# A fused two-block transformer kernel on one core: the gate products of the second block's mixers are spread over the attention, on a ring of six slots

## The chip, the cores and the metric

The kernel runs on one core of a Trainium2 chip. Everything is computed in float32. The metric is the time of one execution in microseconds of the device; the kernel before takes 2779.77 us (median of three runs, 2775.85 to 2779.93).

## The reference, cut to what matters

Two blocks follow each other on 256 tokens of 1024 features. The first (two linear recurrences and a mixture of 32 experts) isn't touched by the change. The second has two layers; each is a feed-forward half step, a mixer and another feed-forward half step. The change lies in the mixer:

```python
h = rmsnorm(x, norm_mix[l])
qa, ka, va, qb_, kb, vb, qc, kc, vc, gate_logits = jnp.split(h @ w_in[l], split_points, axis=-1)
y_a = mixer_a(...)   # 8 heads of 64: q and k normed and rotated (rope), plain softmax
y_b = mixer_b(...)   # 8 heads of 64: relative bias, window mask, and a sink logit in the softmax
y_c = mixer_c(...)   # 4 heads of 2 x 64: p = softmax(first) - lam * softmax(second), values of 128, norm
ys = jnp.stack([y_a, y_b, y_c], axis=2)                              # 3 branches of 512
branches = jnp.einsum('bsnw,nwd->bsnd', ys, w_branch[l])             # 3 x (512 -> 1024)
gates = jax.nn.sigmoid(gate_logits.reshape(b, s, N_BRANCH, D_MODEL)) # 3 x (1024 -> 1024)
merged = jnp.sum(gates * branches, axis=2)
x = x + merged @ w_out[l]
```

## The kernel before, in words

All weights stream from memory in 446 blocks of 1 MB, in the order that `stream_order` (L63) writes down. SyncE loads block i into a slot of a ring of 12 (`place`, L108); it waits on the count `w_used` until TensorE has freed the block that was in the slot. `take` (L491) is TensorE's side: the next block, once it has landed. Six slots are buffers of their own, the other six are one buffer, `ring_late`. Each engine's program is written out by hand, in its own order, with semaphores between them. On ScalarE the helper `act` (L2009) waits for its own result after each instruction.

A float32 matmul of the source is two instructions in the trace, so a product of 128 x 128 weights with 256 columns shows as two matmuls and two weight loads.

The mixer on TensorE (`mixer`, L1101) does, one after the other:

1. The projections: 8 blocks of q and k with 256 columns each (`project`, tiles of two matmul groups in the banks `pj`, which ScalarE copies out), then v from two blocks.
2. The rope of branch A: ScalarE squares q and k, TensorE sums them over a head (`rope_sums`), VectorE scales (`rope_gained`), TensorE rotates (`rope_rotated`), VectorE and ScalarE finish with eight passes over five tiles. The scores wait for the last of them (`rope_done`).
3. The attention: 24 maps of 256 x 256 scores in 20 units (16 units of one map in A and B, 4 units of two maps in C). For unit u TensorE does the scores of u, the transposes of unit u-2 (`turn`, four of 128 x 128, L513) and the values of unit u-3. For each map VectorE copies the scores out of PSUM or adds the bias (L1876, L1879), takes the row maximum (L1881), negates it (L1889), and after ScalarE's two exponentials divides by the sum (L1902). Scores use 64 rows of the array, the values of A and B 64 columns.
4. The norm of branch C (`c_squared`, `c_sums`, `c_variance`, `c_inverse`, `y_ready`).
5. `merge` (L872): for each of 3 branches and 4 pairs of feature tiles one branch tile (8 products of 256 columns) and one gate tile (16 products). ScalarE copies the first and puts the second through the sigmoid, VectorE multiplies and adds.
6. The output product, 4 blocks with 512 columns, into four banks.

The bias tiles (3 MB) are read back from memory by two transfers on ScalarE's queue at the start of each mixer, since their place is used by the feed-forward steps between.

The feed-forward steps (`feed_forward`, L1056) use a seven-product scheme: 11 steps "up" of two blocks each, whose weights VectorE combines partly in place in the ring (`weights_up`, L1676), and 11 steps "down" of one block.

## Time and profile before

| what | us |
|---|---|
| median of the runs | 2779.77 |
| runs shown | 2775.85, 2779.77, 2779.93 |
| span of the profiled execution, first to last instruction | 2773.7 |
| TensorE busy in it | 2550.8 |
| VectorE busy | 1103.4 |
| ScalarE busy | 585.4 |

No total time is given for the profiled execution beside its span; its span lies 6.1 us under the median of the runs. The mixer of the first layer begins at 1449 us of the span and its output product ends at 1784.6 us; that of the second lies between 2217 and 2553 us.

### The profile page before, as it was taken

What the parts mean: (1) busy time and instruction counts of PE and PEld (TensorE: products, weight loads), DVE (VectorE), ACT (ScalarE), POOL (GpSimd) and SP (SyncE); (2) the same over time, 40 slices, a digit from 0 to 9 for tenths busy, and PEclk for the clock granted to TensorE, in tenths of its full rate; (3) what the DMA queues carried; (4) which work ended last, traced back from release to release, by engine and by line L of the source; (5) the groups of instructions that cost most, each with busy time, mean ns of one, the idle gap of its engine ahead of it and who ended that gap; (6) DMA issues with size and microseconds to landing.
All of it is one profiled execution on the core that took longest, in us unless ns stands there. A gap on an engine that the chain in (4) does not pass through costs nothing.

```text
span 2773.7 us, 37722 instructions
## 1 busy us (share of the span) xinstructions
PE 2550.8 (92%) x15259; PEld 1933.4 (70%) x15264; DVE 1103.4 (40%) x2325; ACT 585.4 (21%) x1032; POOL 115.3 (4%) x98
## 2 busy tenths in 40 slices
PE   5999889989799999979999779999999997799998
PEld 2686588868456655549948468699499484586993
DVE  1455445501311111136550831366666507312665
ACT  3632422210211111121011521110100105311000
POOL 0000144300000000000000000000000000000000
PEclk8999999999999999989999889999999998799999
DMA  7126100025499999974444004344344350043340
GB/s 280 62 79 278 54 31 1 1 108 211 157 414 422 422 422 422 422 309 173 178 147 173 30 1 182 152 166 184 142 162 176 144 196 31 1 182 152 153 168 15
DMA packets 74309, 485.50 MB, mean 175 GB/s; under 512 B 7872, under 2 KB 14528, under 8 KB 16704
## 3 DMA queue, kind: packets, MB, share of 16 engines
q1 hardware_dynamic: 65808, 472.46, 42.8%
q10 hardware_dynamic: 8368, 11.14, 1.2%
q8 instruction: 98, 1.61, 0.2%
q14 instruction: 35, 0.29, 0.0%
HBM read 479.38 MB, written 4.19 MB: 174 GB/s over the span
## 4 chain that ended last, share of the span: by engine, by line
PE 82%; DVE 7%; DMA 5%; ACT 3%; issue 2%; SPq 0%; ACTq 0%; DVEq 0%; POOL 0%; POOLq 0%
PE bank L501 80%; DMA ring<-in_stream 5%; ACT arena L2010 2%; PE bank L513 2%; DVE arena L1191 1%; DVE softmax_small L1881 1%; DVE arena L1879 1%; DVE arena L1902 0%; ACT hT L2010 0%; DMA bias_scratch<-arena 0%; ACT ring_late L2010 0%; DVE arena L1449 0%; ACT L2010 0%; DVE softmax_small L1889 0%; DVE arena L1485 0%
## 5 line engine op out<-in xcount | busy, mean ns | idle before, releaser
L501 PE MATMUL bank<-arena 128*128 128x128 f32 (+4 forms) x3864 | 619.5, 318 | 67.8 <-ACT arena L2010 43.1
L501 PEld LDWEIGHTS bank<-arena 128*128 128x128 f32 (+2 forms) x3864 | 485.4, 195 | 175.5 <-issue 87.0
L501 PE MATMUL bank<-hT,ring 128*128 128x256 f32 (+2 forms) x2144 | 463.3, 374 | 8.1 <-issue 6.7
L2010 ACT ACTIVATE arena<-bank 128x512 f32<-128x512 f32 (+2 forms) x384 | 218.0, 568 | 1156.7 <-PE bank L501 1131.2
L501 PEld LDWEIGHTS bank<-hT,ring 128*128 128x128 f32 x2144 | 357.5, 193 | 97.1 <-issue 64.7
L501 PE MATMUL bank<-ring,arena 128*64 128x256 f32 (+3 forms) x2184 | 298.6, 406 | 31.3 <-DMA ring<-in_stream 29.0
L501 PE MATMUL bank<-hT,ring_late 128*128 128x256 f32 (+1 forms) x1568 | 279.4, 336 | 6.7 <-issue 6.7
L501 PEld LDWEIGHTS bank<-ring,arena 128*64 128x64 f32 (+2 forms) x2184 | 176.4, 141 | 144.7 <-issue 82.7
L501 PEld LDWEIGHTS bank<-hT,ring_late 128*128 128x128 f32 x1568 | 248.9, 193 | 31.0 <-issue 7.5
L2010 ACT ACTIVATE hT<-bank 128x256 f32<-128x256 f32 (+2 forms) x92 | 38.6, 420 | 642.4 <-PE bank L501 471.3
L501 PE MATMUL bank<-arena,ring_late 128*128 128x128 f32 (+1 forms) x1088 | 157.4, 299 | 5.1 <-DVE arena L1485 2.8
L501 PE MATMUL bank<-ring_late,hT 128*64 128x512 f32 (+2 forms) x632 | 162.0, 584 | 0.0
L1191 DVE TENSOR_TENSOR arena<-arena 128x512 f32<-128x512 f32 (+5 forms) x55 | 33.7, 615 | 321.4 <-ACT arena L2010 320.8
L501 PEld LDWEIGHTS bank<-arena,ring_late 128*128 128x128 f32 x1088 | 144.2, 193 | 12.7 <-DVE arena L1485 3.6
L513 PE MATMUL bank<-constants,arena 128*128 128x128 f32 x492 | 87.1, 325 | 58.3 <-ACT arena L2010 44.5
L501 PE MATMUL bank<-arena,ring 128*128 128x128 f32 (+1 forms) x864 | 125.0, 299 | 11.5 <-issue 8.0
L513 PEld LDWEIGHTS bank<-constants,arena 128*128 128x128 f32 x492 | 68.1, 167 | 93.1 <-issue 58.0
L1191 DVE TENSOR_TENSOR arena<-arena,bank 128x512 f32<-128x512 f32 x16 | 11.0, 688 | 303.7 <-PE bank L501 303.7
L501 PEld LDWEIGHTS bank<-arena,ring 128*128 128x128 f32 x864 | 114.1, 195 | 17.7 <-issue 12.7
L501 PEld LDWEIGHTS bank<-ring_late,hT 128*64 128x64 f32 (+1 forms) x632 | 58.1, 147 | 87.8 <-issue 85.0
L501 PE MATMUL bank<-ring_late,arena 128*64 128x256 f32 (+2 forms) x680 | 115.7, 404 | 3.2 <-DVE arena L1513 2.3
L2001 POOL TENSOR_TENSOR x_tok<-x_tok,arena 128x512 f32<-128x512 f32 x8 | 11.8, 1492 | 2207.2 <-DVE arena L1802 2207.2
(215 smaller groups left out, 2239.1 us busy)
## 6 DMA issues: line engine op xcount, KB each, us to landing
ring<-in_stream SPq DMA_DIRECT2D x248, 1024.0 KB, 8.9
ring_late<-in_stream SPq DMA_DIRECT2D x198, 1024.0 KB, 10.4
arena<-bias_scratch ACTq DMA_DIRECT2D x4, 1536.0 KB, 18.0
bias_scratch<-arena ACTq DMA_DIRECT2D x12, 256.0 KB, 2.0
constants<-in_con SPq DMA_DIRECT2D x1, 1184.0 KB, 9.3
x_tok<-in_x SPq DMA_DIRECT2D x1, 1024.0 KB, 5.3
arena<-in_ctx SPq DMA_DIRECT2D x1, 1024.0 KB, 6.8
out<-x_tok SPq DMA_DIRECT2D x2, 512.0 KB, 2.7
```

The lines of the kernel that those rows point to most:

```text
L501: ins = engine.matmul(out_, lhsT, rhs, start=start, stop=stop, skip_group_check=True)
L513: ins = engine.transpose(out_, in_, ident[0:k, 0:k])
L1191: return tt(o, x, y, ALU.mult)
L1879: tt(e, src, bias2[:, m.bias], ALU.add).then_inc(*v.inc("sm_in"))
L1881: engine.tensor_reduce(stat(m, 0), e, AX.X, ALU.max).then_inc(*v.inc())
L2001: engine.tensor_tensor(x, x, ffU[j], ALU.add).then_inc(*g.inc("ff_joined"))
L2010: engine.activation(o, i, f, **kw).then_inc(*s_.inc(ev))
```

## The change

Parts of the second block alone are changed.

- **Ring.** From the end of the experts on, blocks go through six slots and not twelve. `ring_slots` makes a table of each block's slot, its use count and the block that was there before it. `ring_late` is free from there on: its first half holds the gates of a mixer (`gates2`, 24 tiles of 256 columns), its second half the bias tiles, which are now loaded once, on ScalarE's queue right behind the experts.
- **Stream.** The order is now all 12 gate blocks, then the 6 branch blocks, then the 4 output blocks.
- **Rope.** It is woven into the projections: sums and rotation stand on TensorE behind the fourth of the eight q and k tiles, and v comes last.
- **Attention.** It goes in 12 steps of two maps. In each TensorE does the scores of both maps, alternating between the two row halves; the first half of one gate tile; the transposes of the step before; the second half of the gate tile; and the values of the step before, alternating between the two column halves. ScalarE copies the gate logits into `gates2`.
- **Softmax.** VectorE takes maximum and bias in one instruction per 128 x 256 half for B and C (`tensor_tensor_reduce`, listed as ISA, with a read of the accumulator), and reduces straight from PSUM for A; the copy and the negation are gone. The sink is a 257th column of the exponential.
- **Branches last.** 12 branch tiles in banks 2 and 3 alternately, multiplied by VectorE straight from PSUM with the gates. The last step's transposes stand behind the first branch tile and its values behind the second. ScalarE does the sigmoids as four instructions of 1024 columns before the norm of C and two behind it.

The diff, cut to its core:

```diff
+def ring_slots():
+    slots = [i % (RING if EARLY <= i < MOE_LAST else HALF_RING) for i in range(N_BLOCKS)]
...
-                    back = HALF_RING if i < EARLY + HALF_RING else RING
-                    if i >= back:
-                        sp.wait_ge(sem("w_used"), i - back + 1)
+                    if before(i) >= 0:
+                        sp.wait_ge(sem("w_used"), before(i) + 1)
...
             def mixer(l, turned):
-                project(8, LAT, turned)
-                w = [take(), take()]
-                project_tok([(lambda k, t_=t_: hT[:, k, NC + 128 * t_:NC + 128 * t_ + 128]) for t_ in range(2)], w)
-                engine.wait_ge(*pe.at("pj_free", state["tile"]))
+                steps = project_steps(8, LAT, turned)
+                for _ in range(3):
+                    next(steps)
                 engine.wait_ge(*pe.at("lam_product", l + 1))
                 mm(bank[7][:, 256:258], ..., ev="lam_sums")
+                next(steps)
...
+                for _ in steps:
+                    pass
+                w = [take(), take()]
+                project_tok([(lambda k, t_=t_: hT[:, k, NC + 128 * t_:NC + 128 * t_ + 128]) for t_ in range(2)], w)
...
+                def scores(t):
+                    pair = MAPS[2 * t:2 * t + 2]
+                    for m in pair:
+                        if m.n >= 3:
+                            scores_free(m.n - 3)
+                    for qb in range(2):
+                        for m in pair:
                             a0, a1 = m.lanes
                             mm(bank[2 + m.n % 3][:, 256 * qb:256 * qb + 256], qT[a0:a1, m.q, 128 * qb:128 * qb + 128],
                                (kc if m.kc else kab)[a0:a1, m.k, :], start=True, stop=True, ev="sm_scores" if qb else None)
...
-                for u in range(N_UNITS + 3):
-                    if u < N_UNITS:
-                        scores(u)
-                    if 2 <= u < N_UNITS + 2:
-                        turn(u - 2)
-                    if u >= 3:
-                        values(u - 3)
+                def branch_tile(i, w):
+                    b, m2 = divmod(i, 4)
+                    if i < 2:
+                        for n in (N_MAPS - 3, N_MAPS - 2, N_MAPS - 1):
+                            scores_free(n)
+                    else:
+                        engine.wait_ge(*pe.at("merge_used", 8 + 12 * l + i - 1))
+                    if b == 2 and m2 == 0:
+                        engine.wait_ge(*pe.at("y_ready", 3 + l))
+                    t = bank[2 + i % 2]
...
+                for t in range(N_SLOTS):
+                    scores(t)
+                    gate = gate_tile()
+                    gate_half(gate, 0)
+                    if t:
+                        turn(t - 1)
+                    gate_half(gate, 1)
+                    if t:
+                        values(t - 1)
+                for b in range(3):
+                    w = [take(), take()]
+                    for m2 in range(4):
+                        if b == 0 and m2 == 1:
+                            turn(N_SLOTS - 1)
+                        if b == 0 and m2 == 2:
+                            values(N_SLOTS - 1)
+                        if b == 1 and m2 == 0:
+                            engine.wait_ge(*pe.at("c_squared", l + 1))
...
+                        branch_tile(4 * b + m2, w)
...
-                    if m.bias is None:
-                        engine.tensor_copy(e, src).then_inc(*v.inc("sm_in"))
...
-                    engine.tensor_reduce(stat(m, 0), e, AX.X, ALU.max).then_inc(*v.inc())
...
+                    for qb in range(2):
+                        engine.tensor_tensor_reduce(e[:, qb, 0:256], src[:, qb, :], bias2[:, m.bias, qb, :], -1.0, sink,
+                                                    ALU.add, ALU.min, stat(m, 0)[:, qb:qb + 1]).then_inc(*v.inc("sm_max" if qb else None))
...
+                def branch_tile(i):
+                    b, m2 = divmod(i, 4)
+                    engine.wait_ge(*v.at("br_full", 12 * l + i + 1))
+                    if i in (0, 8):
+                        engine.wait_ge(*v.at("gates_ready", 2 * l + i // 8 + 1))
+                    o, g, src = mrg2[:, 2 * m2:2 * m2 + 2, :], gates2[:, 2 * i:2 * i + 2, :], psum(2 + i % 2, 2)
...
                 act(csq, y4, ACT.Square, "c_squared")
+                for i in range(4):
+                    act(gates2[:, 4 * i:4 * i + 4, :], gates2[:, 4 * i:4 * i + 4, :], ACT.Sigmoid, "gates_ready" if i == 3 else None)
                 engine.wait_ge(*s_.at("c_variance", l + 1))
                 act(csq, csq, ACT.Ln)
                 act(csq, csq, ACT.Exp, "c_inverse", scale=-0.5)
-                merge(3, 8 + 12 * l, eg2, brs2)
+                for i in range(4, 6):
+                    act(gates2[:, 4 * i:4 * i + 4, :], gates2[:, 4 * i:4 * i + 4, :], ACT.Sigmoid, "gates_ready" if i == 5 else None)
```

How the order of the instructions moves, at three places. The names of the waits are those of semaphores that are used a second time: `gla_scores` is `sm_scores`, `gla_arg` `sm_max`, `gla_exp` `sm_exp`, `gla_products` `sm_p`, `dn_p` `sm_turned`, `dn_p_copied` `sm_pt`, `dn_y` `sm_pv`, `dn_d` `sm_o`; `gla_merged` is `sm_in` before and `br_full` now; `dn_u_copied` is `lam_product`, `dn_at_copied` `rope_squared`, `dn_x0` `lam_read`, `dn_a` `rope_gained`.

TensorE, attention of the first layer, before: one unit of branch A in the steady state.

```order
L501 MATMUL bank4<-arena 128x256 [waits gla_merged]
L501 MATMUL bank4<-arena 128x256
L513 MATMUL bank6<-constants,arena 128x128 [waits dn_p_copied,gla_products]
L513 MATMUL bank6<-constants,arena 128x128 x3
L501 MATMUL bank7<-arena 64x256 [waits dn_d,dn_p_copied]
L501 MATMUL bank7<-arena 64x256
```

The same place now: one step of two maps.

```order
L524 MATMUL bank3<-arena 128x256 [waits gla_exp]
L524 MATMUL bank4<-arena 128x256
L524 MATMUL bank3<-arena 128x256
L524 MATMUL bank4<-arena 128x256
L524 MATMUL bank0<-hT,ring1 128x256 [waits landed1,pj_free]
L524 MATMUL bank0<-hT,ring1 128x256 x7
L536 MATMUL bank5<-constants,arena 128x128 [waits gla_products,dn_p_copied]
L536 MATMUL bank5<-constants,arena 128x128 x3
L536 MATMUL bank6<-constants,arena 128x128 [waits gla_products]
L536 MATMUL bank6<-constants,arena 128x128 x3
L524 MATMUL bank0<-hT,ring1 128x256 x8
L524 MATMUL bank7<-arena 64x256 [waits dn_d,dn_p_copied]
```

Sixteen gate products came between the scores, the transposes and the values, eight on each side of the transposes.

TensorE, from the last attention step of the first layer into the branch tiles, now (bank 2 and bank 3 are the branch tiles):

```order
L524 MATMUL bank2<-hT,ring5 128x256 [waits gla_arg,landed0,landed5]
...
L536 MATMUL bank6<-constants,arena 128x128 [waits gla_products,dn_p_copied]
L536 MATMUL bank6<-constants,arena 128x128 x3
L524 MATMUL bank3<-hT,ring5 128x256 [waits gla_arg]
...
L524 MATMUL bank7<-arena 128x256 [waits dn_d,dn_p_copied]
L524 MATMUL bank7<-arena 128x256
L524 MATMUL bank2<-hT,ring5 128x256 [waits merge_used]
```

The third branch tile stands behind the last values, and it needs the bank of the first.

ScalarE at the same place, now: from the copy of the last transposes (into `arena`) and the last values to the last sigmoids.

```order
L2097 ACTIVATE arena<-bank6 128x512 [waits dn_p,dn_y,dn_d]
L2097 ACTIVATE arena<-bank7 128x256 [waits dn_y,dn_p_copied]
L2097 ACTIVATE arena<-arena 128x1024 [waits dn_d]
ACT_TABLE_LOAD
L2097 ACTIVATE ring_late<-ring_late 128x1024 [waits c_squared]
L2097 ACTIVATE ring_late<-ring_late 128x1024 [waits act] x3
ACT_TABLE_LOAD [waits c_variance]
L2097 ACTIVATE arena<-arena 128x1024 [waits gates_ready]
ACT_TABLE_LOAD
L2097 ACTIVATE arena<-arena 128x1024 [waits act]
ACT_TABLE_LOAD
L2097 ACTIVATE ring_late<-ring_late 128x1024 [waits c_inverse]
```

The four sigmoids behind which `gates_ready` is raised come after the square of branch C, and four table loads stand here; before, the merge had one.

## Rows read from the trace of the kernel before

**Rows 1.** The page: the span, and the busy time of each engine.

```profile
span 2773.7 us, 37722 instructions
PE 2550.8 (92%) x15259; PEld 1933.4 (70%) x15264; DVE 1103.4 (40%) x2325; ACT 585.4 (21%) x1032; POOL 115.3 (4%) x98
```

**Rows 2.** Busy time of the engines in stretches: the first layer's mixer, and some of the second's.

```profile
core 0: us, PE busy (x) PEld busy (x) DVE busy (x) ACT busy (x) POOL busy (x), PEclk, DMA share, GB/s
1449.00:1518.40 69.40, 69.30 (x323) 60.69 (x320) 0.94 (x3) 6.14 (x11) 0.00 (x0) 1.00 0.54 197
1518.40:1535.30 16.90, 7.74 (x14) 3.73 (x14) 9.99 (x16) 4.82 (x6) 0.00 (x0) 0.76 0.34 124
1535.30:1617.20 81.90, 64.31 (x256) 37.67 (x256) 64.94 (x172) 50.01 (x144) 0.00 (x0) 0.82 0.00 1
1617.20:1627.00 9.80, 1.98 (x4) 0.68 (x4) 4.02 (x7) 3.17 (x3) 0.00 (x0) 0.79 0.00 0
1627.00:1640.00 13.00, 12.95 (x46) 10.96 (x47) 0.00 (x0) 0.60 (x1) 0.00 (x0) 0.77 0.01 1
1640.00:1756.80 116.80, 114.58 (x531) 100.51 (x529) 13.84 (x20) 16.31 (x25) 0.00 (x0) 1.00 0.33 133
```

**Rows 3.** The chain that ended last: start us, us, what.

```profile
1570.86 0.70 DVE arena L1879
1571.58 0.70 DVE softmax_small L1881
1574.21 0.70 DVE arena L1879
...
1627.05 127.54 PE bank L501 x576
...
1756.85 27.75 PE bank L501 x64
...
2217.22 69.08 PE bank L501 x320
...
2525.06 27.75 PE bank L501 x64
```

**Rows 4.** Groups by form in the attention, 1535.4 to 1617 us.

```profile
L2010 ACT ACTIVATE arena<-arena,softmax_small 128x256 f32<-128x256 f32 x48 | 24.4, 508 | 25.1 <-DVE softmax_small L1889 24.1
L1902 DVE TENSOR_SCALAR arena<-arena,softmax_small 128x256 f32<-128x256 f32 x40 | 14.1, 353 | 1.4
L2010 ACT ACTIVATION_READ_ACCUMULATOR arena<-arena,softmax_small 128x1 f32 x48 | 9.0, 187 | 0.0
L1898 DVE RECIPROCAL softmax_small<-softmax_small 128x2 f32<-128x2 f32 x24 | 4.0, 166 | 1.2 <-ACT arena L2010 0.5
L1909 DVE SCALAR_TENSOR_TENSOR arena<-arena,softmax_small 128x256 f32<-128x256 f32 x8 | 3.9, 485 | 0.3
```

**Rows 5.** TensorE (PE: matmul, PEld: weight load), 1582 to 1592 us: start, us, engine.

```profile
1581.94 2.13 PE L501 MATMUL bank<-arena 128*64 128x256 f32 x8 [0.36 <-ACT arena L2010]
1584.28 0.66 PE L513 MATMUL bank<-constants,arena 128*128 128x128 f32 x4 [0.20 <-DVE arena L1902]
1588.64 2.15 PE L501 MATMUL bank<-arena 128*64 128x256 f32 x12 [0.36 <-ACT arena L2010]
1582.95 0.73 PEld L501 LDWEIGHTS bank<-arena 64*128 64x128 f32 x4 [0.39 <-issue]
1589.65 0.74 PEld L501 LDWEIGHTS bank<-arena 64*128 64x128 f32 x8 [0.39 <-issue]
```

**Rows 6.** ScalarE, 1617 to 1645 us.

```profile
1616.80 0.38 ACT L2010 ACTIVATE arena<-bank 128x256 f32<-128x256 f32 x1 [0.76 <-PE bank L501]
1617.22 1.06 ACT L2010 ACTIVATE arena<-arena 128x1024 f32<-128x1024 f32 x1
1640.70 1.28 ACT L2010 ACT_TABLE_LOAD   x1 [6.27 <-PE bank L501]
1641.99 0.60 ACT L2010 ACTIVATE arena<-bank 128x512 f32<-128x512 f32 x1
```

**Rows 7.** VectorE, two feed-forward steps up of the first layer's second feed-forward.

```profile
1805.79 1.29 DVE L1687 TENSOR_TENSOR arena<-ring_late 128x512 f32<-128x512 f32 x2
1818.29 1.28 DVE L1687 TENSOR_TENSOR arena<-ring_late 128x512 f32<-128x512 f32 x2
```

**Rows 8.** DMA issues of the weight stream, 1784 to 1990 us: KB each, median us to landing.

```profile
ring<-in_stream SPq DMA_DIRECT2D x16, 1024.0 KB, 4.9
```

More of the change, by code:

```diff
@@ L105, with before @@
 EARLY, HALF_RING = 48, 6
+def ring_slots():
+    slots = [i % (RING if EARLY <= i < MOE_LAST else HALF_RING) for i in range(N_BLOCKS)]
+    last, table = {}, []
+    for i, slot in enumerate(slots):
+        before, uses = last.get(slot, (-1, 0))
+        table.append((slot, uses + 1, before))
+        last[slot] = i, uses + 1
+    return table
+SLOTS_OF = ring_slots()
 def place(i):
-    if i < EARLY:
-        return i % HALF_RING, i // HALF_RING + 1
-    slot = i % RING
-    return slot, i // RING + 1 + (EARLY // RING if slot < HALF_RING else -(EARLY // RING))
+    return SLOTS_OF[i][:2]
+def before(i):
+    return SLOTS_OF[i][2]
 LEVELS_1 = LEVELS + 1
@@ L478, in _ @@
                 sp.wait_ge(sem("ov_used"), 3 * 6 * EXPERTS)
-            load_range(MOE_LAST, N_BLOCKS)
+            for i in range(MOE_LAST, N_BLOCKS):
+                load(i, place(i)[0])
             for j in range(2):
@@ L1157, in mixer, with gate_tile, gate_half @@
-                engine.wait_ge(*pe.at("c_squared", l + 1))
-                for j in range(2):
-                    mm(bank[2 + j][:, :], ones[:, 0:128], csq[:, 2 * j:2 * j + 2, :], start=True, stop=True,
-                       ev="c_sums" if j else None)
+                def gate_tile():
+                    return pj_tile(), take()[:, :].rearrange("p (m k c) -> p m k c", m=2, k=KT)
+                def gate_half(gate, m):
+                    o, w = gate
+                    for k in range(KT):
+                        end = m == 1 and k == KT - 1
+                        mm(o[:, 256 * m:256 * m + 256], w[:, m, k, :], hT[:, k, LAT], start=k == 0, stop=k == KT - 1,
+                           ev="pj_full" if end else None, frees=int(end))
@@ new lines, in turn @@
+                def turn(t):
+                    engine.wait_ge(*pe.at("sm_pt", nu + UNITS_BY[t]))
+                    for i, u in enumerate(SLOT_UNITS[t]):
+                        engine.wait_ge(*pe.at("sm_p", nu + u + 1))
+                        b = bank[5 + (i if len(SLOT_UNITS[t]) == 2 else t % 2)]
+                        for qb in range(2):
+                            for sb_ in range(2):
+                                transpose(b[:, 256 * sb_ + 128 * qb:256 * sb_ + 128 * qb + 128],
+                                          E_[UNITS[u].maps[0].n % 4][:, qb, 128 * sb_:128 * sb_ + 128],
+                                          ev="sm_turned" if qb and sb_ else None)
@@ new lines, in values @@
+                def values(t):
+                    engine.wait_ge(*pe.at("sm_pt", nu + UNITS_BY[t + 1]))
+                    engine.wait_ge(*pe.at("sm_o", ns + t))
+                    units = [UNITS[u] for u in SLOT_UNITS[t]]
+                    for sb_ in range(2):
+                        for i, unit in enumerate(units):
+                            a0, a1 = unit.out
+                            mm(bank[7][a0:a1, 0:256], vt[:, sb_, unit.v:unit.v + a1 - a0],
+                               PT[i if len(units) == 2 else t % 2][:, sb_, :], start=sb_ == 0, stop=sb_ == 1,
+                               ev="sm_pv" if sb_ and i == len(units) - 1 else None)
@@ new lines, in branch_tile @@
+                def branch_tile(i, w):
[8 more added lines that the diff above has]
+                    t = bank[2 + i % 2]
+                    for m in range(2):
+                        for k in range(4):
+                            wk = w[k // 2][:, :].rearrange("p (k c) -> p k c", k=2)
+                            end = m == 1 and k == 3
+                            mm(t[:, 256 * m:256 * m + 256], wk[:, k % 2, 256 * m2 + 128 * m:256 * m2 + 128 * m + 128],
+                               yl[4 * b + k], start=k == 0, stop=k == 3, ev="br_full" if end else None,
+                               frees=2 if end and m2 == 3 else 0)
@@ new lines, in mixer @@
+                for t in range(N_SLOTS):
[16 more added lines that the diff above has]
+                            engine.wait_ge(*pe.at("c_squared", l + 1))
+                            for j in range(2):
+                                mm(bank[4 + j][:, :], ones[:, 0:128], csq[:, 2 * j:2 * j + 2, :], start=True, stop=True,
+                                   ev="c_sums" if j else None)
+                        branch_tile(4 * b + m2, w)
```

231 lines of the change are left out of this document (114 added, 117 removed).

## The prediction

> **What bounds the kernel now.** I read the page first: TensorE is busy for 2550.8 of 2773.7 us [rows 1], so only its idle time and its slow stretches can be won by reordering. Then the stretches of the first mixer [rows 2], then the chain of waits [rows 3], then the groups and single instructions in the attention [rows 4, 5]. What they show:
>
> [...]
> - Rope: 16.9 us in which TensorE has 14 instructions and works 7.7 us at a clock of 0.76.
> - Attention: 81.9 us. VectorE is busy for 64.9 and the chain runs VectorE, VectorE, one map every 3.35 us (1570.86 to 1574.21) [rows 3]. TensorE is counted busy for 64.3, but at clock 0.82, in bursts.
> - Norm of branch C: 9.8 us with 2 us of TensorE.
> - Merge: 129.8 us, full of TensorE work. The first 13 us hold 46 matmuls at clock 0.77; from there it is 531 in 114.6 us, 0.216 us each [rows 2].
> - Output product: 27.8 us [rows 3].
>
> From the first projection to the output product that is 1449.0 to 1756.8, 307.8 us; the second layer has 2217.2 to 2525.1, 307.9 [rows 3]. Of the 288 float32 products of the merge (576 instructions) two thirds, the gates, depend on neither rope nor attention. The change puts them where TensorE waits for VectorE.
>
> **The new mixer, part by part, on TensorE.**
>
> *Projections and rope.* Still 69.4 us. The rope's 12 instructions (8 of 512 columns, 4 of 256) now stand behind the fourth tile. At full clock 512 columns take 27.75 / 64 = 0.434 us [rows 3], 256 take 0.216: 8 x 0.434 + 4 x 0.216 = 4.3 us, with 0.6 for the lambda product and exposed weight loads 4.9. Nothing waits: the squares and gains that they need follow the third tile and take under 3 us on ScalarE and VectorE (1.06 us for 1024 columns [rows 6]), and the fourth tile lasts 32 x 0.216 = 6.9. The passes that end the rope took VectorE under 10 us [rows 2] and have four tiles and v, over 40 us. If that cover were gone, the 12 us by which the old rope was longer than this would be back.
>
> *Attention with gates.* Gates: 12 tiles of 32 instructions, 384 x 0.216 = 82.9 us. Transposes: 20 units at 0.66 [rows 5], 13.2. Scores: one unit's four instructions follow the values 1.01 us behind (1581.94 to 1582.95), and values and scores together take 2.13 us. In branch C, values and the eight score instructions of two maps on the two row halves take 2.15 [rows 5]: eight as long as four. So a step's eight scores cost 1.1 us, 13.2 for twelve. Values: one unit's four instructions 1.0 us; a pair on the two column halves I take as 1.05, as the row halves do, 12.6 for twelve. Changes of kind, where a weight load waits and isn't hidden (the load stands still for 0.39 us at each such change, of which about 0.15 reaches the matmuls since four of 0.216 fill 0.86 of the 1.01 us) [rows 5]: some two more a step, 3.6. Sum 125.5 us, 10.6 a step for A and B.
>
> Does anyone else need longer? VectorE per step of B: two small copies, four fused operations with four reads of the accumulator, two reciprocals (the small ones at 0.17 each) and four scalings of 0.353 [rows 4]. The fused operation isn't in the trace; between 0.353 (a one-input pass of that size) and twice 0.485 (the two-input pass, if the reduction halved its rate) I take 0.5, as the two-input pass is nearest. That makes 8 x 0.17 + 4 x 0.353 + 4 x 0.5 = 4.8 us, at the upper bound 6.7, both under 10.6. ScalarE: four exponentials of 0.51 and four reads of 0.19 [rows 4], two transposed tiles and a gate tile of 0.60, one output of 0.38 [rows 6]: 5.0 us. The chain from the scores through maximum, exponentials and scaling to the transposes takes 6 to 8 us and has a whole step plus half a gate tile. So TensorE is the bound, with no gap, and at 1.00 clock as in the projections.
>
> *Branches.* 192 x 0.216 = 41.5 us, the sums for the norm of C 4 x 0.434 = 1.9 with a load. Here I see **one new wait**. The third branch tile needs bank 2, which VectorE frees once it has multiplied the first by the gates; it waits for `gates_ready`, and ScalarE raises that only behind the last values: copy 0.42, square 1.06, table load 1.28, four sigmoids of 1.06, then the product 0.69, with 0.4 for handing over [rows 3, 6]. That is 8.1 us in which TensorE stands. Queued behind it are all later tiles; nothing else is there to run. After 9.8 us of near idleness the old merge ran its first 13 us at 0.77, 46 instructions where 13 / 0.216 = 60 fit: 3.0 us lost [rows 2]. I take 3.0 again, with 0 (clock held) and 6 (twice that) as ends. `y_ready` isn't late, by an estimate from the same rows: the six tiles and the sums up to the ninth tile take 6 x 3.46 + 1.9 = 22.7 us behind the wait; VectorE has the sixth tile done at 17, and four scalings of 0.5 and a pass of 0.7 make it 20. ScalarE's root with its two table loads lies within that.
>
> [...]
>
> *End.* Product, addition, hand-over: 1.7 us.
>
> *The ring of six.* A feed-forward step up takes 12.5 us [rows 7] and two blocks. The six slots hold three steps. A pair of blocks is asked for at the end of step s-2; VectorE wants it in step s, TensorE in step s+1, 12.5 and 25 us later, and a block lands in 4.9 us [rows 8]. That costs nothing. The steps down use a block in 14 x 0.434 = 6.1 us, the output in 6.9, gates and branches more slowly: nothing either. The bias transfers move behind the experts, where TensorE waits for VectorE's sums anyway, and their second copy is gone: nothing either way.
>
> **Sum.** 69.4 + 4.9 + 125.5 + 41.5 + 1.9 + 8.1 + 3.0 + 1.7 = 256.0 us against 307.8: 51.8 saved a layer, 103.6 for two. The span would be 2670.1. Runs stood 6.1 us over the profiled span at the median, so 2676.
>
> **Rivals.**
>
> 1. *TensorE's step is longer.* If row halves didn't overlap, eight scores cost 4 x 0.216 more, 0.86 x 24 = 21 us; if each of three changes of kind a step cost the whole 0.39 and not 0.13, another 0.26 x 3 x 24 = 19 us. Together 2716. For it: alternating between halves is a new order. Against: eight took as long as four. [...] Chance 0.19.
> 2. *The softmax side stays the bound.* If the fused operation took 2.5 us, VectorE would need 2.8 + 4 x 2.5 = 12.8 us a step in B and C, 2.2 more than TensorE, in 16 steps of both layers: 2711. No two-input pass in the trace is that slow. Chance 0.06.
> 3. *The long idle is cheaper,* because the clock holds and the gaps between kinds are hidden by the gate products: 3.0 + 3.6 less a layer, 2663. Chance 0.10.
> 4. *Slower than before: the half ring starves the feed-forward.* A pair is asked for three steps ahead and not six. If a pair took over 23 us to land (25, less 4 x 1.3 for VectorE [rows 7], plus some 3.6 of products that don't need its result), each of 44 steps up would wait. The change loses from 2.4 us a step on, since 44 x 2.4 is the gain; at 27 us of landing it is 44 x 4 = 176, giving 2852. Against it are 4.9 us. Chance 0.03.
> 5. *It doesn't do what it says:* the gate products stand in the attention in the written order, and only a wait I overlooked could push them out. Then about the old time. Chance 0.01.
>
> **How the numbers follow.** The forecast, 2676, has 0.61. Its own range is 2660 to 2697 (clock 0 to 6 a layer, changes of kind free to double, wait 7 to 10). Rivals 1 and 2 reach to 2716, rival 3 to 2663. The range 2655 to 2718 leaves out rival 4, rival 5 and tails. A measurement of this kernel can tell about 0.2%, 5.6 us, from no change. Faster 0.95, same 0.01, slower 0.04.
>
> **What would show it.** Right: TensorE over 97% busy at clock 1.00 from the first projection to the first branch tile, some 200 us long; a step of 10 to 11 us; no stall at the rope; one idle stretch of about 8 us behind the last values, ended by VectorE and ScalarE's sigmoids, with a slow clock behind it. The feed-forward stretches keep their length and TensorE never waits for a landing. Wrong: TensorE idle within the steps on VectorE or ScalarE, steps over 11.5 us, waits of TensorE on DMA in the feed-forward, or a wait on `y_ready` at the ninth branch tile.

## The result, and the profile after

| | before | after |
|---|---|---|
| median of the runs, us | 2777.81 | 2649.23 |
| lowest to highest, us | 2773.29 to 2779.93 (4 runs) | 2649.09 to 2650.08 (4 runs) |
| span of the profiled execution, us | 2773.7 | 2647.3 |
| one mixer, first projection to output product, us | 307.8 | 247.1 |

The ratio is 0.9544 [0.9533, 0.9556]: 128.6 us faster, where 103.6 (2676 in all) was forecast. The time lies 6 us under the low end of the range.

The page of the profile after, against [rows 1]:

```profile
span 2647.3 us, 36938 instructions
PE 2483.6 (94%) x15264; PEld 1894.7 (72%) x15264; DVE 1049.6 (40%) x2294; ACT 581.0 (22%) x994; POOL 115.5 (4%) x98
```

TensorE does the same matmuls. Its busy time fell by 67.2 us; the other 59 us of the span were idleness. Only a part of the 67.2 is the lower clock of stretches that are gone. This is a stretch in the attention of the kernel before, with the columns of [rows 2]:

```profile
1575.00:1585.00 10.00, 8.37 (x36) 4.66 (x36) 9.06 (x28) 7.10 (x22) 0.00 (x0) 1.00 0.00 0
```

The clock is 1.00 here, and still the eight value and score instructions of one map take 2.13 us [rows 5]. Now sixteen of two maps take 2.08 (the step below), since two maps share the array on its halves. By these two numbers the pairing gives 8 x (2 x 2.13 - 2.08) = 17 us a layer, an estimate of about half of the 67.2. The rest, transposes and clock, wasn't taken apart.

The gain is also seen by stage. Busy time of the engines in stretches of the first mixer, after, with the columns of [rows 2]; they are projections with rope, attention with gates, the new wait, and the branches:

```profile
1444.90:1518.00 73.10, 73.10 (x334) 62.87 (x333) 10.19 (x20) 10.06 (x15) 0.00 (x0) 1.00 0.40 144
1518.00:1643.80 125.80, 125.79 (x675) 101.53 (x673) 39.20 (x156) 52.22 (x140) 0.00 (x0) 1.00 0.33 118
1643.80:1651.80 8.00, 0.00 (x0) 0.00 (x0) 0.71 (x2) 6.95 (x7) 0.00 (x0) 0.64 0.00 0
1651.80:1692.00 40.20, 38.67 (x164) 32.62 (x164) 16.51 (x26) 9.36 (x8) 0.00 (x0) 0.94 0.29 105
```

For 198.9 us TensorE is never idle and its clock is 1.00. VectorE and ScalarE do the softmax beside it with time to spare: 39.2 and 52.2 of 125.8 us, where VectorE had 64.9 of 81.9 in [rows 2]. The chain of waits, after (start us, us, what), shows what is left:

```profile
1444.94 86.47 PE bank L524 x398
...
1643.89 0.39 ACT arena L2097
...
1644.30 1.06 ACT arena L2097
1645.38 1.28 ACT L2097
1646.67 1.06 ACT ring_late L2097
...
1651.09 0.70 DVE arena L1271
...
1651.84 38.67 PE bank L524 x164
1690.51 1.56 issue
1692.07 27.72 PE bank L524 x64
```

From 1444.94 to 1643.80 the chain is TensorE and nothing else, in pieces of which the first is shown. Then come the predicted steps in the predicted order: copy, square, table load, four sigmoids, product. The second mixer runs from 2151.66 to 2398.70, 247.0 us.

One step of the attention with its gate tile, as TensorE's timeline of the kernel after has it (start us, us, engine, line, operation):

```profile
1581.55 1.04 PE L536 MATMUL bank<-constants,arena 128*128 128x128 f32 x8
1582.42 3.62 PE L524 MATMUL bank<-hT,ring 128*128 128x256 f32 x16
1585.97 2.15 PE L524 MATMUL bank<-arena 128*64 128x256 f32 x16
1588.05 3.72 PE L524 MATMUL bank<-hT,ring 128*128 128x256 f32 x16
1591.60 1.04 PE L536 MATMUL bank<-constants,arena 128*128 128x128 f32 x8
```

Transposes, half a gate tile, eight value and eight score instructions, the other half: 10.05 us from one row of transposes to the next. Each piece is listed with an end 0.07 to 0.17 us behind the start of the next, so a piece is read from start to start: the eight transposes take 0.87 us, the halves of the gate tile 3.55, values and scores together 2.08.

### The profile page after: what moved, and what is told of

It is laid out like the page before. It is cut to its first block, busy times and chain, and to the rows that moved or that the text cites. A ratio compares the mean times of both kernels' runs of the same rounds, so it can differ in the third digit from the quotient of the medians.

```text
span 2647.3 us, 36938 instructions
## 1 busy us (share of the span) xinstructions
PE 2483.6 (94%) x15264; PEld 1894.7 (72%) x15264; DVE 1049.6 (40%) x2294; ACT 581.0 (22%) x994; POOL 115.5 (4%) x98
## 4 chain that ended last, share of the span: by engine, by line
PE 89%; DVE 3%; ACT 3%; DMA 2%; issue 1%; SPq 0%; ACTq 0%; POOL 0%; DVEq 0%; POOLq 0%
PE bank L524 87%; PE bank L536 2%; DMA ring<-in_stream 2%; ACT arena L2097 2%; DVE arena L1271 1%; ACT ring_late L2097 1%; ACT hT L2097 0%; ACT L2097 0%; DVE arena L1529 0%; DVE arena L1565 0%; DMA bias_scratch<-arena 0%; ACT small L2097 0%; DVE x_tok L1887 0%; DVE arena L1533 0%; DVE x_tok L1629 0%
## 5 line engine op out<-in xcount | busy, mean ns | idle before, releaser
L524 PE MATMUL bank<-hT,ring 128*128 128x256 f32 (+2 forms) x3712 | 741.5, 358 | 17.7 <-DVE arena L1271 16.1
L524 PEld LDWEIGHTS bank<-hT,ring 128*128 128x128 f32 x3712 | 598.4, 192 | 136.0 <-issue 65.0
L2097 ACT ACTIVATE arena<-bank 128x512 f32<-128x512 f32 (+1 forms) x336 | 189.3, 563 | 967.2 <-PE bank L524 917.4
L524 PE MATMUL bank<-arena,ring 128*128 128x128 f32 (+1 forms) x1664 | 224.8, 293 | 11.6 <-issue 8.0
L524 PEld LDWEIGHTS bank<-arena,ring 128*128 128x128 f32 x1664 | 211.6, 193 | 20.2 <-issue 12.7
L524 PE MATMUL bank<-ring,hT 128*128 128x256 f32 (+1 forms) x368 | 124.8, 481 | 0.0
L536 PE MATMUL bank<-constants,arena 128*128 128x128 f32 x492 | 75.5, 302 | 48.1 <-ACT arena L2097 43.2
L524 PE MATMUL bank<-ring_late,hT 128*64 128x512 f32 x512 | 113.4, 595 | 0.0
L524 PE MATMUL bank<-hT,arena 128*128 128x128 f32 x704 | 85.8, 275 | 0.0
L524 PE MATMUL bank<-arena,hT 128*128 128x512 f32 x176 | 82.7, 592 | 0.0
L524 PEld LDWEIGHTS bank<-hT,arena 128*128 128x128 f32 x704 | 82.1, 192 | 0.0
## 6 DMA issues: line engine op xcount, KB each, us to landing
bias_scratch<-arena ACTq DMA_DIRECT2D x12, 256.0 KB, 2.0
```

The source lines that it names most:

```text
L524: ins = engine.matmul(out_, lhsT, rhs, start=start, stop=stop, skip_group_check=True)
L536: ins = engine.transpose(out_, in_, ident[0:k, 0:k])
L2097: engine.activation(o, i, f, **kw).then_inc(*s_.inc(ev))
```

## The experiments

**1. The order of the halves.** The first doubt was whether pairs of maps overlap on the row and column halves only because the change writes them alternately. This kernel writes the scores map by map and the values unit by unit.

```diff
-                    for qb in range(2):
-                        for m in pair:
+                    for m in pair:
+                        for qb in range(2):
...
-                    for sb_ in range(2):
-                        for i, unit in enumerate(units):
+                    for i, unit in enumerate(units):
+                        for sb_ in range(2):
```

> The changed kernel with the pairing undone: scores map by map, values unit by unit. Theory A (TensorE overlaps the two halves whatever the order within the step, since the old branch C ran eight score instructions in the time of four without alternation): within 0.2% of the changed kernel, 2649. Rival B (only neighbours in the order overlap): scores and values cost up to 0.86 us more each, steps of 11.8 us in A and B, up to 24 x 0.86 + 16 x 0.86 = 34 us more, 2683.

Measured: 2651.2 us, ratio 0.9556 [0.954, 0.9572]; the step is as long as before. TensorE's timeline of this kernel:

```profile
1560.66 1.04 PE L536 MATMUL bank<-constants,arena 128*128 128x128 f32 x8
...
1565.08 2.16 PE L524 MATMUL bank<-arena 128*64 128x256 f32 x16
...
1570.73 1.04 PE L536 MATMUL bank<-constants,arena 128*128 128x128 f32 x8
```

Here two products in a row on the same half (four instructions of the trace), with as many for the other half behind them, cost nothing: the sixteen value and score instructions take 2.16 us, and 2.15 in the kernel after. The alternate order of the change isn't what makes its step short. That two maps stand in one step is, by the 2.13 us that one map alone took in the kernel before [rows 5].

**2. The changes of kind.** Four gate products between the scores of the two query blocks put two more changes into each step.

```diff
-                    scores(t)
+                    scores(t, (0,))
...
-                    gate_half(gate, 0)
+                    gate_half(gate, 0, range(4))
+                    scores(t, (1,))
+                    gate_half(gate, 0, range(4, 8))
```

> The changed kernel with four gate products put between the scores of the first and the second query half: two more changes of kind a step, 48 in all, and two instruction groups of four score instructions where there was one of eight. Theory A (a change costs little where full products stand on both sides): 48 x 0.1 = 5 us more. Rival B (each change costs what the prediction's bound had, 0.39 us): 48 x 0.39 = 19 us more, 2668.

Measured: 2661.08 us, ratio 0.9586 [0.957, 0.9602]. TensorE's timeline of this kernel:

```profile
1556.93 1.04 PE L536 MATMUL bank<-constants,arena 128*128 128x128 f32 x8
...
1561.35 1.72 PE L524 MATMUL bank<-arena 128*64 128x256 f32 x12
1563.00 1.99 PE L524 MATMUL bank<-hT,ring 128*128 128x256 f32 x8
1564.92 0.70 PE L524 MATMUL bank<-arena 64*128 64x256 f32 x4
1565.55 1.99 PE L524 MATMUL bank<-hT,ring 128*128 128x256 f32 x8
1567.38 0.82 PE L536 MATMUL bank<-constants,arena 128*128 128x128 f32 x6
```

The step is 10.45 us, 0.40 more, so one more change of kind costs 0.2 us: between the 0.13 of the forecast and the 0.39 of rival 1. Over 24 steps that is 9.6 us, and the median is 11.9 higher. Part of it is that short groups overlap less: the four scores that now stand alone take 0.63 us from start to start, where half of eight would be 0.54 (eight alone take 1.07 in the first step of the kernel after, 1518.46 to 1519.53).

**3. The gates behind the attention.** All twelve gate tiles are computed after the last values; the two maps per step stay. ScalarE's copies of the gate logits move with them, behind its square of branch C.

```diff
-                    gate = gate_tile()
-                    gate_half(gate, 0)
...
-                    gate_half(gate, 1)
-                    if t:
...
+                turn(N_SLOTS - 1)
+                values(N_SLOTS - 1)
+                for t in range(N_SLOTS):
+                    gate = gate_tile()
+                    gate_half(gate, 0)
+                    gate_half(gate, 1)
```

> The changed kernel with all gate tiles taken out of the attention and put behind it; pairing, fused softmax, woven rope and branches last stay. Theory A (the gain is the gates filling TensorE's idle time; the softmax chain still sets the attention alone at about 6.5 us a step): attention of 70 to 80 us and 83 us of gates behind it, 2 x 40 us more, 2725 to 2745. Rival B (the fused softmax and the pairs made the attention itself short, about 45 us): only 2 x 10 us more, 2670.

Measured: 2762.45 us, ratio 0.9957 [0.994, 0.9973]; 113 us over the kernel after and higher than every theory had it. Busy time of the engines in the attention of the first mixer, and two pieces of TensorE's timeline there, of this kernel:

```profile
1519.60:1615.10 95.50, 56.82 (x251) 34.30 (x247) 39.07 (x156) 44.59 (x128) 0.00 (x0) 0.70 0.06 22
```

```profile
1562.86 3.98 PE L524 MATMUL bank<-arena 128*64 128x256 f32 x16 [3.88 <-ACT arena L2095]
...
1571.75 3.98 PE L524 MATMUL bank<-arena 128*64 128x256 f32 x16 [3.40 <-ACT arena L2095]
```

Without gate products between them the two-map steps take 95.5 us, more than the 81.9 of the kernel before [rows 2]. No engine is full: VectorE works 39 of 95.5 us and ScalarE 45. It is a round trip. This step is 8.9 us (1562.86 to 1571.75; the mean of twelve is 8.0): values and scores at a clock of 0.50 (sixteen instructions in 4.0 us that take 2.1 in the kernel after at 1.00), maximum, exponentials, and behind these, in ScalarE's order, the copies of the transposes for which the values and next scores wait. Round trip and clock together are why the run came out above what was expected. So the change's attention by itself is slower than the old one; it wins because gate products cover all of it but TensorE's own time, which is short since two maps share the array. The 95.5 us and 85.95 us behind them, the gates with the last four value instructions, make 181.5, against 118.4 for both in the kernel after. Of these 63 us a layer, 7 come back: the two branch tiles now run while the sigmoids do. From the first projection to the third branch tile it is 1445.48 to 1708.19, 262.7 us, against 206.9.

**4. The rope behind all projections**, where it stood before, with the rest of the change.

```diff
-                for _ in range(3):
-                    next(steps)
+                for _ in steps:
+                    pass
```

> The changed kernel with the rope put back behind all projections, gates in the attention as they are. Theory A (the woven rope removed a stall that the trace of before shows as 16.9 us with 4.5 of work, and a slow clock behind it): 12 us a layer plus 3 for the clock, 30 us more, 2679. Rival (the first gate tiles and the fused order cover it): under 10 us more.

Measured: 2678.3 us, ratio 0.9646 [0.963, 0.9662], 29 us over the kernel after. The chain of waits of this kernel:

```profile
1447.57 69.48 PE bank L524 x320
...
1519.55 4.12 PE bank L524 x6
...
1531.69 15.51 PE bank L524 x64
```

The projections end at 1517.05 and TensorE's next long stretch begins at 1531.69: 14.6 us. The rope's twelve matmuls lie in them, for which the kernel after needs 4.3 us (1472.63 to 1476.93), so the cover saves 10.3. Behind it the clock is low again (0.83 from 1531.69 to 1547.20; 64 instructions in 15.51 us, 13.8 at 0.216), and the later stretch of branches is 0.75 us longer. That makes 12.8 of the 13.9 us by which the mixer is longer here (1447.57 to 1708.59, 261.0 against 247.1). The cover that the prediction priced at 12 us is worth 10 to 11, and a slow clock comes on top.

**5. The ring alone.** The kernel before with six slots from the second block on and nothing else.

```diff
+    slots = [i % (RING if EARLY <= i < MOE_LAST else HALF_RING) for i in range(N_BLOCKS)]
...
-                    back = HALF_RING if i < EARLY + HALF_RING else RING
-                    if i >= back:
-                        sp.wait_ge(sem("w_used"), i - back + 1)
+                    if before(i) >= 0:
+                        sp.wait_ge(sem("w_used"), before(i) + 1)
```

> The kernel before with one part of the change alone: six ring slots, not twelve, from the end of the experts on; nothing else. Theory A (a pair of blocks lands in about 5 us and has 12 to 25): same as before, ratio 1.000 +- 0.002, the feed-forward stretches 198 us as before and TensorE never waiting for a landing. Rival (the ring does something: either it starves the feed-forward, or its other load pattern is where the 4 us ahead of the first mixer came from): slower by over 5 us with TensorE waiting on DMA, or faster by about 4 us with the second block starting at 1233 us and not 1237.

Measured: 2802.24 us, ratio 1.0095 [1.0079, 1.0112]: 27 us slower than the kernel before. The feed-forward isn't where it went, and this was in neither theory. The chain of waits of this kernel, the merge of the first mixer and the feed-forward behind:

```profile
1627.68 38.91 PE bank L517 x167
1666.58 8.96 DMA ring<-in_stream
...
1714.47 8.94 DMA ring<-in_stream
...
1770.15 29.30 PE bank L517 x64
...
2019.51 198.53 PE bank L517 x1374
```

TensorE's timeline of this kernel at the ends of those two landings:

```profile
1675.67 14.60 PE L517 MATMUL bank<-hT,ring 128*128 128x256 f32 x54 [3.51 <-DMA ring<-in_stream]
```

The old merge holds the six blocks of a branch and frees nearly all of them in its last gate tile (`frees=0 if m2 < 3 else 5`). With six slots the next branch's blocks are asked for only when this one's come free, and land 8.9 us later; TensorE has work for 5.5 of them and stands for 3.5. Twice a layer it stands (3.49 us the second time), and runs at a low clock behind (0.50 from 1675.67 to 1680, 0.81 over the 14.60 us of the row above): from the merge's start to the output product it is 1627.68 to 1770.15, 142.5 us against 129.8 in [rows 3], and the output product takes 29.3 against 27.75. That is 14.2 us a layer, 28 in all. The feed-forward keeps its length. So six slots "cost nothing" only together with the new stream order, in which a gate tile or a branch tile needs and frees few blocks at a time. The trace of the kernel before had this wait already: its first block goes through six slots and has the same merge, and between the two branches there TensorE stands for the same 3.5 us:

```profile
614.77 5.38 PE L501 MATMUL bank<-arena,ring 128*128 128x256 f32 x16 [3.48 <-DMA ring<-in_stream]
```

**6. Four slots in the second block** of the kernel after.

```diff
-    slots = [i % (RING if EARLY <= i < MOE_LAST else HALF_RING) for i in range(N_BLOCKS)]
+    slots = [i % (HALF_RING if i < EARLY else RING if i < MOE_LAST else 4) for i in range(N_BLOCKS)]
```

> The changed kernel with four ring slots and not six in the second block. Theory A (what bounds the ring is only how soon a freed pair lands, 5 to 6 us of the 12.5 us of a step; the 27 us of six slots in the old kernel came from its merge, which frees six blocks at once): within 10 us of 2649, the feed-forward stretches at most 2 us longer. Rival (the ring is near its edge at six): VectorE's combination of the weights comes late in each of 44 steps up, over 2 us each, 90 us more, 2740.

Measured: 2651.74 us, ratio 0.9559 [0.9543, 0.9575], no different from the kernel after. One feed-forward stretch in the chain of this kernel, and the weight stream between 1725 and 1920 us (KB each, median us to landing):

```profile
1938.13 198.74 PE bank L524 x1374
```

```profile
ring<-in_stream SPq DMA_DIRECT2D x31, 1024.0 KB, 4.8
```

The kernel after has 198.53 us for that stretch. The feed-forward ahead of it is 2.6 us longer than there, from its start to the next one's 1722.44 to 1938.13 (215.7) against 1726.79 to 1939.91 (213.1). TensorE waits for no landing in it, and the difference lies behind its last instruction there, where it waits 7.86 us for ScalarE and not 5.45; why stays open. Rival 4 is refuted with a margin: even four slots, two steps' worth of blocks, are enough while a block lands in 4.8 us and a step lasts 12.5.

**7. The fused operation undone.** Bias and sign by one pass over 512 columns, then a reduction, then the sink; as before the change.

```diff
-                        for qb in range(2):
-                            engine.tensor_tensor_reduce(e[:, qb, 0:256], src[:, qb, :], bias2[:, m.bias, qb, :], -1.0, 1e30,
-                                                        ALU.add, ALU.min, stat(m, 0)[:, qb:qb + 1]).then_inc(*v.inc("sm_max" if qb else None))
+                        stt(e[:, :, 0:256], src, -1.0, bias2[:, m.bias], ALU.mult, ALU.subtract).then_inc(*v.inc())
+                        engine.wait_ge(*v.last())
+                        engine.tensor_reduce(stat(m, 0), e[:, :, 0:256], AX.X, ALU.min).then_inc(*v.inc("sm_max"))
```

> The changed kernel with the fused bias and maximum of branches B and C taken apart again: one pass over 512 columns that adds the bias and turns the sign, one reduction, and for B one small pass with the sink. Theory A (TensorE alone sets the step of 10.06 us, VectorE has 5 us of slack in it): within 0.2% of 2649, with steps of 10.06 us. Rival B (VectorE's share of the chain shows through in-order waits): 0.5 us more in each of 32 steps of B and C of both layers less the first, some 8 to 16 us more.

Measured: 2652.6 us, ratio 0.9558 [0.9542, 0.9574]; the step stays at 10.06 us. (The 32 of the expectation are maps, in 16 steps; its price for rival B is by the map.) The trace of the kernel after lists the `tensor_tensor_reduce` of one half as two instructions, and neither under the name ISA: `CUSTOM_DVE_ANT_0`, 480 ns, and `DVE_READ_ACCUMULATOR2_ANT`, 84 ns, in the second branch; in the third (L1954) they take 421 and 83 ns. The groups of the second branch there, 1518 to 1643.8 us, sixteen of each for its eight maps, and VectorE's timeline of this experiment:

```profile
L1962 DVE CUSTOM_DVE_ANT_0 arena<-bank,ring_late,softmax_small 128x256 f32<-128x256 f32 x16 | 7.1, 480 | 0.0
...
L1962 DVE DVE_READ_ACCUMULATOR2_ANT softmax_small<- 128x1 f32 x16 | 1.3, 84 | 0.0
```

```profile
1589.12 0.68 DVE L1961 SCALAR_TENSOR_TENSOR arena<-bank,ring_late 128x512 f32<-128x512 f32 x1
1589.84 0.69 DVE L1963 TENSOR_REDUCE softmax_small<-arena 128x2 f32<-128x512 f32 x1
1590.56 0.23 DVE L1965 TENSOR_SCALAR softmax_small<-softmax_small 128x2 f32<-128x2 f32 x1
```

Fused, a map costs VectorE 2 x (0.48 + 0.08) = 1.12 us; apart, 1.60. The fusion saves VectorE half a microsecond a map and the kernel nothing, since VectorE isn't waited for.

**8. The sigmoids earlier.** The prediction's one new wait, taken away. On ScalarE the four sigmoids go ahead of the copy of the last transposes, so that they run beside TensorE's first branch tiles.

```diff
+                    else:
+                        for i in range(4):
+                            act(gates2[:, 4 * i:4 * i + 4, :], gates2[:, 4 * i:4 * i + 4, :], ACT.Sigmoid, "gates_ready" if i == 3 else None)
...
-                for i in range(4):
-                    act(gates2[:, 4 * i:4 * i + 4, :], gates2[:, 4 * i:4 * i + 4, :], ACT.Sigmoid, "gates_ready" if i == 3 else None)
```

> The changed kernel with the four sigmoids of the first sixteen gate tiles moved ahead of ScalarE's copy of the last transposes, under the first branch tile. Theory A (the 8 us stall is ScalarE's chain behind the last values, and the slow clock of some 2 us behind it comes with the stall): both go in both layers, 20 us less, 2629. Rival B (the wait only moves: the copy of the last transposes now comes late and the last values wait): 2 x 5 us less at most, 2640. Rival C: the clock stays slow for another reason, 16 us less, 2633.

Measured: 2630.55 us (2627.77 to 2632.6), ratio 0.9481 [0.9465, 0.9497]. The chain of waits of this kernel, and one stretch of it from the first projection to the end of the branches:

```profile
1638.92 40.57 PE bank L524 x184
1679.48 1.55 issue
1681.04 27.72 PE bank L524 x64
```

```profile
1444.40:1679.50 235.10, 235.09 (x1170) 195.52 (x1169) 65.27 (x201) 78.61 (x170) 0.00 (x0) 1.00 0.34 126
```

The mixer is 1681.04 - 1444.39 = 236.65 us, 10.5 shorter: 8.05 for the wait, and 2.4 for the clock, which now stays at 1.00. That prices the slow clock behind the wait by itself. The median is 18.7 us under the kernel after, where twice 10.5 is 21.

**9. The output product by pairs.** Experiment 8, and the output product waits for each pair of merged tiles rather than for all four.

```diff
-                engine.wait_ge(*pe.at("merged", 2 + l))
...
+                    engine.wait_ge(*pe.at("merged", 2 + 4 * l + j2))
...
-                    tt(o, o, mtmp2[i % 2], ALU.add).then_inc(*v.inc("merged" if i == 11 else None))
+                    tt(o, o, mtmp2[i % 2], ALU.add).then_inc(*v.inc("merged" if i >= 8 else None))
```

> The changed kernel with the early sigmoids of e3 and, in addition, the output product waiting for each pair of merged tiles alone (four waits) and not for the last one before it begins. Theory A: the idle 1.56 us before the output product goes in both layers, 3 us less than e3. Rival: the wait only moves behind the first block of the output product; since that takes 6.9 us, that can't be seen. Expected 2627 against e3's 2630, and about 0.946 of the kernel before.

Experiment 8 ran again beside it:

> The kernel of e3 once more, on the same chip as e10: 2626 to 2632, 3 us above e10 if the four waits do what they should; 0 to 1 us if the spread of the part ahead of the second block hides them.

Measured, against a kernel before of 2775.03 us: 2625.06 us (2624.22 to 2630.58, 5 runs), ratio 0.9462 [0.945, 0.9475]; experiment 8 again 2627.55 us, ratio 0.9467 [0.9454, 0.948]. The chain of waits of experiment 9:

```profile
1637.51 0.44 PE bank L536 x4
1637.94 68.05 PE bank L524 x248
```

The 1.55 us ahead of the output product are gone (68.05 us is less than 40.57 + 27.72). The medians differ by 2.5 us, where the chain has 3.1 less; by the runs alone the two can't be told apart. From the start of the second block to the end of the span, experiment 8 has 1393.4 us in both of its profiles and experiment 9 has 1390.9. The medians of the two lie 19 to 24 us under the kernel after.

**10. The kernel before once more,** unchanged, for the spread of what lies ahead of the second block.

> The kernel before, unchanged, profiled a second time. If the 4 us by which the second block began later in the first profile of before is a spread of the experts (where the weight stream sets the pace at the end), this profile begins the second block at another time between 1229 and 1238 us, and its span minus that start is within 1 us of the first profile's (2773.7 - 1237.1 = 1536.6). Rival (the change moved something ahead of the second block): it begins at 1237 again.

Measured: 2775.87 us against 2775.03, ratio 0.9999 [0.999, 1.0009]. Its second block began at 1236.23 us, span 2775.2. The start was expected to vary; it did so by 0.9 us between two profiles of this kernel. What was expected to stand still didn't: from that start to the end it is 1539.0 us, 2.4 more than in the first profile, where under 1 was expected.

## Why the prediction was right in its mechanism and too high in its number

- **What bounds it: right.** TensorE is full from projection to first branch tile at clock 1.00. The table has the terms for the first layer, in us.

| term | forecast | measured |
|---|---|---|
| projections and rope | 69.4 + 4.9 = 74.3 | 73.5 |
| attention with gates | 125.5 | 118.4 (125.3 less two branch tiles, 32 x 0.216) |
| the wait for the sigmoids | 8.1 | 8.0 |
| branches, sums, clock, end | 48.1 | 47.1 |
| sum | 256.0 | 247.1 |

- **The step that failed is the attention's sum, above all its "Transposes: 20 units at 0.66".** That row [rows 5] holds the time up to its listed end, not the time until the next piece starts. Eight among the gate products take 0.87 us from start to start, 0.44 a unit: 8.8 us and not 13.2. TensorE's timeline of the kernel before has units with no wait behind them too:

```profile
1560.64 0.65 PE L513 MATMUL bank<-constants,arena 128*128 128x128 f32 x4
1561.23 2.13 PE L501 MATMUL bank<-arena 128*64 128x256 f32 x8
```

  From start to start that is 0.59. So 0.07 of the 0.22 is how the row was read, and 0.15 goes with the neighbours: half-array instructions there, full-array gate products here. It may be that the price of a unit held part of a change of kind, and that the sum had it twice; no run took this apart. Values with scores take 2.08 us in eight steps and 2.02 in two of branch C, with 1.07 twice for scores alone and 0.86 and 1.04 for values alone: 24.7 and not 25.8. For "some two more a step, 3.6", the changes of kind, 118.4 - 82.9 - 8.8 - 24.7 leaves 2.0. So 4.4 of the 7.1 us are the transposes, 1.1 values and scores, 1.6 the changes. All three terms erred the same way. Experiment 2 shows that two changes more cost 0.4, so the 0.3 was a fair price for changes put in anew; the ones in the step are cheaper than that.
- **The offset was wrong.** "Runs stood 6.1 us over the profiled span at the median" was added to the new span. Every run of every kernel here is 1.8 to 2.3 us longer than its own span, and here the median stands 1.9 over the profiled one (2649.2 against 2647.3). The other 4.2 was the distance of one execution to the median of others, and it doesn't carry over to another kernel.
- **Sizes of the miss.** 2 x 8.9 in the mixers, 4.2 from the offset, and 5.0 outside the mixers: 27 us. Of the 5.0, 4.1 lie ahead of the second block, which began at 1233.03 where it was 1237.14. The code there is the same. In the other profiles with the new ring table this start lay between 1228.9 and 1235.2 (1235.2 in experiment 2), in the kernel before at 1236.2 and 1237.1. Two pieces make most of the 4.1. The output product of the first block took 27.9 us and not 29.5. And in the last experts the weight stream sets the pace at 29.7 us an expert, where TensorE's own pace is 28.95: for the last four in the profile before, for one after. Both vary among kernels that are alike there; experiment 2 has 29.5 and four. So spread can account for it; whether the new ring has a share stays open.
- **The new wait and `y_ready`: right.** Table load and sigmoid follow each other as in [rows 6]: the sigmoid at 1646.67 stands 0.01 us behind the end of the 1.28 us load at 1645.38. The forecast had 8.1 + 3.0 = 11.1 us a layer for wait and clock; experiment 8 took both away and its mixer is 10.5 shorter. The range let the wait be up to 10 us; no run shows that: it is 8.05 here and in experiments 1, 2, 4, 6 and 7.
- **The slow clock: right mechanism.** The first 13 us behind the wait ran at clock 0.83 and show 46 matmuls, as many as in [rows 2]:

```profile
1651.80:1664.80 13.00, 12.96 (x46) 10.33 (x47) 3.25 (x5) 0.23 (x1) 0.00 (x0) 0.83 0.13 35
```

  The 0.83 is a mean: 0.50 for the first 4.2 us, then 0.97 and 1.00. A trace can miss a few matmuls (15259 are in that of the kernel before [rows 1], 15264 in that of the kernel after, which does the same ones), so the loss is better read from the whole stretch: 38.67 us where 160 x 0.216 + 4 x 0.434 = 36.3 would do, 2.4 lost and not 3.0. Experiment 8 gives the same 2.4.

- **VectorE's fused operation: right** (0.42 and 0.48 us against 0.5, experiment 7), and without weight.
- **"The ring of six costs nothing": right, for a reason the text left out.** It looked at the feed-forward alone. Experiment 5 shows that the merge was the place that could have paid, 14 us a layer, and the first block's merge in the trace of before showed the wait.
- **The range.** Its terms add up to 2693 at the top (3.0 + 3.6 + 1.9 a layer over 2676), not 2697; this changes nothing at the low end, where the time fell.
- **Rivals.** 1 was half right on its price (0.2 for one more change), wrong on the overlap and on the total. 2 and 4 are refuted by experiments 7 and 6, 5 by the step shown above, which has the gate products where they are written. 3 had the gaps hidden, as they mostly were, and the clock holding, which it didn't. Its 2663 was nearer than the forecast, and it had 0.10.

## What to carry to other kernels

Fill a latency-bound stretch with work that depends on none of it, and cost the result by the rate of the engine that is then full: durations read from start to start, from groups that stand among the neighbours they will have, not from a short group up to its listed end. Add to a new span only what lies outside every span, not one execution's distance to a median. When a buffer ring is cut, look at who holds slots longest before freeing any, not only at who uses them fastest, and look for a place in the old trace that already runs on the short ring.

## What the runs showed of the hardware

- **What a short group of TensorE instructions costs depends on its neighbours and on how it is read.** Four float32 transposes of 128x128 show 0.66 us up to their listed end [rows 5] and 0.59 from start to start between half-array instructions; among full-array ones eight take 0.87 from start to start, 0.44 for four.
- **Halves overlapped in both orders that were run.** Sixteen value and score instructions on half arrays take 2.15 us with the halves alternating product by product and 2.16 with two products in a row on one half, where full-array instructions of that size take 0.216 each, 3.46 us for sixteen.
- **What idling costs TensorE.** Behind 8.05 us of idleness it runs at 0.83 for the next 13 us, 0.50 for the first 4.2 of them; in experiment 8, where it never stands still, it keeps 1.00 for 235.1 us; in experiment 3, where it stands still for 2.9 to 3.9 us in each step but the first, it gets 0.70 over the attention, and sixteen value and score instructions take 3.2 to 4.0 us instead of 2.1. The kernel before stood for 0.2 to 0.7 us at a time between 1555 and 1590 us and kept 1.00.
